# Two weight panels split earlier in a chain of two transformer blocks: a fifth query panel ahead of the first norm's root, a second memory panel ahead of the compressions' activation

## The reference

```python
def _rmsnorm(x, g):
    xf = x.astype(jnp.float32)
    y = xf * lax.rsqrt(jnp.mean(xf * xf, axis=-1, keepdims=True) + RMS_EPS)
    return (y * g.astype(jnp.float32)).astype(x.dtype)

def _compress(kv, pos, w1, w2):
    ...
    blocks = kv[:, idx] + pos[None, None, :, None, :]
    hid = jax.nn.gelu(jnp.einsum('bnlgd,lde->bnge', blocks, w1))
    return jnp.einsum('bnge,ed->bngd', hid, w2)

def _nsa_mixer(h, w_in, gate_b, cmp_pos, cmp_w1, cmp_w2):
    proj = h @ w_in
    q, kc, vc, ks, vs, kw, vw, gl, q_mem = _split(
        proj, [MIX_WIDTH] + [KV_WIDTH] * 6 + [3 * MIX_HEADS, MEM_WIDTH])
    ...
    kc_b = _compress(kc, cmp_pos[0], cmp_w1[0], cmp_w2[0])
    vc_b = _compress(vc, cmp_pos[1], cmp_w1[1], cmp_w2[1])

def _mem_attention(q_mem, mem_n, w_kv):
    k, v = jnp.split(mem_n @ w_kv, 2, axis=-1)
    ...

def first_block(x, mem, ...):
    for i in range(DEPTH):
        hn = _rmsnorm(x, norm1[i])
        mn = _rmsnorm(mem, norm_mem[i])
        ...
```

## Time and profile before

| what | us |
|---|---|
| median of 3 runs | 2215.55 |
| the 3 runs | 2217.01, 2210.09, 2215.55 |
| the profiled execution | 2217.38 |
| its span in the trace | 2215.6 |
| TensorE busy in the span | 2087.2 (94%) |
| VectorE busy | 1132.5 (51%) |
| ScalarE busy | 829.7 (37%) |
| GpSimd busy | 275.7 (12%) |

### The profile page before, as it was taken

One profiled execution on the slowest core, in us unless ns is written; L12 is line 12 of the kernel. 1 busy time (PEld: TensorE's weight loads), 2 busy tenths in 40 slices (PEclk: granted clock), 3 DMA queues, 4 the chain that ended last, 5 costly groups with the idle time before them and its releaser, 6 DMA issues.

```text
span 2215.6 us, 36210 instructions
## 1 busy us (share of the span) xinstructions
PE 2087.2 (94%) x15473; PEld 1136.2 (51%) x15617; DVE 1132.5 (51%) x1744; ACT 829.7 (37%) x1350; POOL 275.7 (12%) x343
## 2 busy tenths in 40 slices
PE   6988989999999999899999999999998989999998
PEld 3556554444444344689844444454565435444444
DVE  4866764544423457655545454333746465555221
ACT  4334764322322574332242223333435335322122
POOL 2221331000001110222210000011012123000000
PEclk9999999999999999999999999999999999999999
DMA  5442002433223311100024332331420021333220
GB/s 138 129 140 58 2 1 77 114 104 105 95 87 102 96 58 59 39 23 4 4 72 112 103 95 91 128 124 58 133 76 20 20 76 41 112 102 107 95 95 38
DMA packets 203843, 173.61 MB, mean 78 GB/s; under 512 B 20416, under 2 KB 179332, under 8 KB 203684
## 3 DMA queue, kind: packets, MB, share of 16 engines
q1 hardware_dynamic: 202778, 170.34, 25.2%
q10 hardware_dynamic: 906, 0.96, 0.2%
HBM read 169.18 MB, written 2.10 MB: 77 GB/s over the span
## 4 chain that ended last, share of the span: by engine, by line
PE 81%; DVE 8%; ACT 6%; issue 3%; POOL 1%; ACTq 0%; DMA 0%; DVEq 0%; POOLq 0%
PE banks L1142 45%; PE banks L1189 17%; PE banks L1464 5%; PE banks L1243 1%; ACT w_hi L1750 1%; PE banks L1476 1%; DVE w_lo L2317 1%; PE banks L1263 1%; PE banks L1204 1%; PE banks L1221 1%; PE banks L1652 1%; ACT arena L1852 1%; PE banks L1576 1%; POOL arena L990 1%; ACT arena L2151 1%
## 5 line engine op out<-in xcount | busy, mean ns | idle before, releaser
L1142 PE MATMUL banks<-arena,w_hi 128*128 128x512 bf16 (+3 forms) x2099 | 613.9, 373 | 7.8 <-DVE arena L2337 5.3
L2317 DVE TENSOR_TENSOR w_lo<-wring,w_hi 128x2048 bf16<-128x2048 f32 (+3 forms) x162 | 357.5, 2208 | 466.7 <-ACT w_hi L1750 463.0
L1750 ACT ACTIVATE w_hi<-wring 128x2048 f16<-128x2048 f32 (+3 forms) x162 | 294.8, 1822 | 442.4 <-PE banks L1189 255.3
L1142 PE MATMUL banks<-arena,w_lo 128*128 128x512 f16 (+1 forms) x1080 | 403.3, 373 | 3.2
L1189 PE MATMUL banks<-arena,w_hi 128*128 128x512 f16 (+1 forms) x1179 | 353.7, 379 | 2.2 <-DVE arena L2609 1.1
L1142 PEld LDWEIGHTS banks<-arena,w_hi 128*128 128x128 f16 x2160 | 211.0, 98 | 253.8 <-DVE arena L2337 8.2
L990 POOL TENSOR_TENSOR arena<-arena,ntmp 128x512 f32<-128x512 f32 (+1 forms) x79 | 101.9, 1290 | 1252.3 <-ACT ntmp L1780 1246.0
L1189 PE MATMUL banks<-arena,w_lo 128*128 128x512 f16 x608 | 230.4, 379 | 2.0
L1142 PE MATMUL banks<-h_hi,w_hi 128*128 128x512 f16 (+1 forms) x576 | 221.0, 384 | 9.8 <-DVE w_lo L2317 8.4
L1142 PE MATMUL banks<-h_hi,w_lo 128*128 128x512 f16 (+1 forms) x576 | 220.1, 382 | 2.2 <-issue 0.2
L1142 PE MATMUL banks<-h_lo,w_hi 128*128 128x512 bf16 (+1 forms) x537 | 205.4, 382 | 0.0
(11 more groups left out here) (404 smaller groups left out, 2737.1 us busy)
## 6 DMA issues: line engine op xcount, KB each, us to landing
wring<-in_w_ffn_in SPq DMA_DIRECT2D x88, 512.0 KB, 4.8
wring<-in_w_ff SPq DMA_DIRECT2D x32, 1024.0 KB, 5.2
wring<-in_w_ffn_out SPq DMA_DIRECT2D x20, 1024.0 KB, 5.0
wring<-in_rw_w_in SPq DMA_DIRECT2D x11, 1024.0 KB, 5.1
wring<-in_w_in SPq DMA_DIRECT2D x11, 1024.0 KB, 5.0
wring<-in_nsa_w_in SPq DMA_DIRECT2D x7, 1024.0 KB, 5.1
wring<-in_w_mem_kv SPq DMA_DIRECT2D x4, 1024.0 KB, 5.3
wring<-in_w_o SPq DMA_DIRECT2D x4, 1024.0 KB, 5.0
```

The lines of the kernel that those rows point to most:

```text
L1142: last = mm(v, p[0], p[1], start=(i == 0), stop=(i == len(prods) - 1))
L1750: A(w_hi[:, at[0] % NSPLIT, 0:w["size"]], wring[:, w["slot"], 0:w["size"]], ACT.Copy).then_inc(split_hi, 1)
L2317: V.tensor_tensor(w_lo[:, sl, 0:w["size"]], wring[:, w["slot"], 0:w["size"]], w_hi[:, sl, 0:w["size"]], ALU.subtract).then_inc(split_lo, 1)
```

## The change

The fifth query panel (split 4) is brought ahead of the root on both engines: ScalarE's `split_to(NBANK - 1)` ahead of `root(n1a)` becomes `split_to(NBANK)`, and VectorE gets a `split_to(NBANK)` ahead of its wait for `d_root`. The fifth query tile is computed in bank 7, and is put in `own_bank`, the list of tiles that don't wait in `opened`. The second memory panel (split 9) is brought ahead of the compressions' gelu, on ScalarE and on VectorE.

```diff
                 t, mm, v = feature_tile(w, 0, P, hT, "v")
+                if len(nsa_jobs) == NBANK:
+                    t.bank, v = 7, bank[7][:]
+                    mm = [(v, mm[0][1])]
                 nsa_jobs.append((t, mm, [x[:, gp * 3 + r, :] for x in qT], v, qscale[:, gp * 3 + r:gp * 3 + r + 1]))
...
-        own_bank = [conv_jobs[0][0]]
+        own_bank = [nsa_q[NBANK][0], conv_jobs[0][0]]
...
             act.wait_ge(cols_ready, 1)
-            split_to(NBANK - 1)
+            split_to(NBANK)
             root(n1a).then_inc(d_root, 1)
...
             prepare(mem_norm[1], lambda k: None)
-            split_to(mem_jobs[0][0][0].split)
+            split_to(mem_jobs[0][0][0].split + 1)
             for j in range(2):
                 act.wait_ge(gelu_in, j + 1)
...
                 last.then_inc(cmp_pos, 1)
+            split_to(NBANK)
             dve.wait_ge(d_root, n1a["r"] + 1)
             plain(nsa_q)
...
-            split_to(mem_jobs[0][0][0].split)
+            split_to(mem_jobs[0][0][0].split + 1)
             for j in range(2):
                 t = cmp_hid[j]
```

## The result

| what | us |
|---|---|
| kernel before, median of 5 runs | 2213.29 (2210.09 to 2217.01) |
| changed kernel, median of 5 runs | 2200.18 (2199.02 to 2205.11) |
| ratio, with its 95% interval | 0.9944 [0.9928, 0.9960] |
| profiled execution of the changed kernel, its span | 2201.43, 2199.4 |

The changed kernel is faster by 0.56%, 12.4 us of 2213. Two further series of 5 runs of the changed kernel, beside 24 and 21 of before, gave 0.9958 [0.9945, 0.9970] and 0.9960 [0.9947, 0.9973]. All 15 runs of it have a mean of 2202.45 (2199.02 to 2207.49), all 65 of before that were taken for this study 2212.90 (2209.14 to 2217.78): a difference of 10.4 us, uncertain by 1.8.

The account below looks back on a forecast made before the run. TensorE, busy 94% of the span, was taken to bound with two stops over 6 us, VectorE pacing between them. Gains 3.3 + 5.8 less 0.9 for clock gave 8.2 us: 2215.55 - 8.2 = 2207.4, range 2202 to 2213.

Parts of the forecast that it names:

- What bounds, and the order of pacing: TensorE's matmuls and stops bound; VectorE paces 68.28 to 89.24 us, TensorE from 123.40 on.
- First gain: Split 4 ahead of the root: VectorE starts the compression stretch earlier, 3.3 us gained.
- the second stop: TensorE's 6.35 us wait for `w_lo` of split 9, ahead of the first layer's memory value tile.
- Second gain: Split 9 ahead of the gelu: the second layer's first key tile starts 5.8 us earlier.
- The clock, -0.9: Deduction of 0.9 us for a possible 1.2 GHz stretch behind the gap ahead of the second layer's key tile.
- first stop: TensorE's 6.32 us wait for `w_lo` of split 4, ahead of the fifth query tile.
- The base, 2215.55: Median of the kernel before's three runs, spanning 6.9 us, from which the gain was subtracted.
- (1) Half the gain lost: Longer low stretch at the first compression tile, another behind the second gap, late panel: gain 3.9 us, 2211.7; chance 0.20.
- (2) Doesn't reach the end: Downstream low stretches, attention's lead or the next wait eat the gain: 0 to 3 us, 2214; chance 0.10.
- (3) A late landing: Second memory panel lands late, holding ScalarE, gelu and root; landing at 119 would give 2224; chance 0.03.
- (4) More than expected, 11.1: Early load, no low level after either gap, one downstream low stretch gone: gain 11.1 us, 2204.5; chance 0.07.

Follow-up runs that it names:

- the first part alone: Kernel before plus split 4 ahead of the root on both engines and the fifth query tile in bank 7, split 9 unmoved: ratio 0.9981.
- the bank alone: Kernel before with only the fifth query tile in bank 7 and its entry in `own_bank`, no split moved: ratio 0.9996.
- the split alone: Kernel before with split 4 ahead of the root on both engines, the fifth query tile left in bank 1: ratio 0.9985.
- the second part alone: Kernel before with only split 9 moved ahead of the gelu on ScalarE and VectorE: ratio 0.9978.
- before, with idle matmuls: Kernel before with 24 and 26 more matmuls, results unread, filling TensorE's two long stops, no wait moved: ratio 0.9976.
- one split further: Changed kernel with split 10 also ahead of the gelu on both engines: ratio 0.9971 against the kernel before.

## Why the prediction missed by little: point by point

**What bounds, and the order of pacing: right.** VectorE fills the compression stretch (20.51 of 20.98 us) as before, and its row at 64.24 shows no wait for TensorE. Behind the second stop TensorE is busy for all of 74.00 us.

**First gain: right.** Forecast 3.3; the trace shows 3.3, and the first part alone gave 4.2 [2.2 to 6.2 by its interval]. The gap ahead of the sixth tile was to be 2.7 and is 2.77. It did bring the low level to part of the sixth tile (0.63 us for a 512-column matmul from 52.06 to 54.62, where 0.38 is usual), and as forecast VectorE's chain hid it.

**Second gain: right.** Forecast 5.8, in the trace 6.0, alone 4.9 by the runs (2.7 to 7.1). The landing wait was to be 0.6 and is 0.57; the gelu starts 2.4 us behind the end of rest 8 for 2.6; the gap ahead of the second layer's key tile was to be 1.9 and is 1.71. Only the length of the low stretch that it removes was taken from too few rows (under "The clock"). By the Trainium skill, SBUF — State Buffer, section "SBUF: two separate sides", rest 9 might have been held behind a GpSimd selection. It wasn't: ScalarE released it, it started 0.19 us behind rest 8 and took 2.29 us. GpSimd's pair of selections, which started behind it, took 2.45 us, for 0.52 beside the gelu's operations; that agrees with the section, by which the one that starts second waits:

```profile
100.86 2.45 POOL L1016 TENSOR_SCALAR_AFFINE_SELECT masks<-masks 64x32 f32<-64x32 f32 x2
...
104.83 0.52 POOL L1016 TENSOR_SCALAR_AFFINE_SELECT masks<-masks 64x32 f32<-64x32 f32 x2
```

**The clock, -0.9: wrong, the first step that failed.** It was meant for a low stretch behind the second gap. Neither the trace above nor those of the two repeats (gaps of 1.92 and 1.49 us) has one there; the windows from the key tile on for 74 us show 1.00 in all three. It also left out that the low stretch which the change removes has no fixed length. I took the value tile's 6.6 us, 1.4 over the 5.2 of the full level, from one trace. Behind the same stop it takes 6.82 us with the first part alone, 7.89 with the bank alone, and 7.88 with the split alone:

```profile
112.66 0.37 PE L1142 MATMUL banks<-w_hi,arena 128*128 128x256 f16 x1 [6.35 <-DVE w_lo L2317]
...
120.54 0.38 PE L1142 MATMUL banks<-arena,w_hi 128*128 128x256 f16 x2
```

So it costs 1.4 to 2.7 us, 2.1 on the mean of these four traces. Without the deduction the sum is 9.1, with the trace's second gain 9.3, with this mean some 10.0; the runs say 10.4, uncertain by 1.8.

Nothing behind the second stop is shown to add to it. Each trace cut at the second layer's first key tile:

| kernel | the key tile starts at, us | from there to the span's end, us |
|---|---|---|
| before | 123.40 | 2092.2 |
| the bank alone | 123.67 | 2087.0 |
| the split without the bank | 120.54 | 2087.0 |
| the first part alone | 119.62 | 2087.4 |
| before, with idle matmuls | 119.77 | 2084.5 |
| the second part alone | 116.98 | 2086.5 |
| the changed kernel, three traces | 113.39, 113.92, 113.16 | 2086.0, 2089.1, 2086.2 |

The lead of 10.0 us is there at the key tile. Counted from the root, without what the starts differ by, it is 9.3 to 10.4 us (79.24 us in before and 80.20 with the bank alone, for 69.77 to 70.17 in the changed kernel's three), and that is all of the 10.4 of the runs. Behind it the changed kernel's three traces average 2087.1 us, no less than the kernels that keep one or both of the old stops; the trace of before is the one that stands apart. The mean granted clock is higher in the changed kernel, 0.9849 over 15 runs against 0.9822 over 60 of before, but that lies ahead of the key tile. The windows up to it, of before and of the changed kernel, and one of before's first stop:

```profile
0.00:123.40 123.40, 93.66 (x463) 58.21 (x468) 78.77 (x107) 47.95 (x77) 40.47 (x118) 0.90 0.51 131
0.00:113.39 113.39, 91.73 (x468) 57.39 (x468) 76.02 (x105) 48.52 (x78) 35.67 (x100) 0.95 0.53 133
44.20:50.40 6.20, 0.00 (x0) 0.00 (x0) 3.38 (x5) 4.01 (x8) 0.00 (x0) 0.80 0.00 0
```

A clock of 0.90 over 123.40 us is 12.3 us short of full, 0.95 over 113.39 is 5.7: the 6.7 between them are 0.003 of the span, all of the difference. Part of it is in the stops themselves, where the clock is already low (0.80) and TensorE has nothing to run.

**The base, 2215.55: the step that cost most.** I took the median of three runs as the place of the kernel before. Among 65 runs it lies high: their mean is 2212.9, and 8 of them are at 2215.5 or more. The three later series were run on three chips, with means of 2212.1, 2213.1 and 2213.4 for before. The profiled execution of before, 2217.38, is higher still, which is why the two traces differ by 16.2 us and not by 10: of the 6.2 us that come up behind 123.40, some 5 belong to that one execution (2092.2 for 2087.0 in the table). The repeats' traces lead it by 12.6 and 16.2 us at the end, and by 9.5 and 10.2 at the key tile.

The miss of 7.2 us thus comes apart into 2.7 from the base (2215.55 - 2212.90), 2.2 from the gain (10.4 for 8.2: 0.9 the deduction for the clock, 0.2 the second gain, some 0.7 the low stretch that is longer in other traces, and 0.4 within what the runs leave uncertain), and 2.3 since the first five runs lie below the mean of all fifteen (2202.45 - 2200.18), which is luck of the draw. My range left the first and the last out: it was made from the cases' sizes around a base that I treated as known to a us, where three runs that span 6.9 us say it isn't.

**The rivals.** (1) Half the gain lost: the longer low stretch, the second gap's and a late landing all failed to come. (2) Doesn't reach the end: it does, 10.0 us at 123.40 were not given back. (3) A late landing: 0.57 us in the changed kernel; the mechanism is real, as one split further shows. (4) More than expected, 11.1: nearest to the 12.4 of the first five runs, by another way; the load landed no earlier, the first gap did bring the low level, and no low stretch downstream is shown to have dropped out. Of its conditions only the second gap at the full level came true.

## What to carry to other kernels

When an engine waits for a reduction of another, move into that wait the operation that its consumer will want next, and then look for the same operation in the queue of every engine that makes it: here the split's new place gave the gain, and the free bank nothing that could be told. Stop where the load of the moved step isn't certain to be there, because everything queued behind it, and every bank that this work frees, waits with it. Take the price of a low stretch from several traces, since one trace shows one length of it, and compare traces at the end of the changed stretch before the rest of a span is put down to a change. Before a gain of a few us is forecast as a time, learn how far runs of the old kernel spread, and put that into the range.

## What the runs showed of the hardware

The spread of one kernel's runs goes with TensorE's granted clock. Of 60 runs of before, by the mean clock of each:

| mean granted clock | runs | mean time, us |
|---|---|---|
| 0.980 | 3 | 2215.43 |
| 0.981 | 14 | 2215.18 |
| 0.982 | 22 | 2212.77 |
| 0.983 | 11 | 2211.33 |
| 0.984 | 9 | 2210.38 |
| 0.985 | 1 | 2211.53 |

A fit gives 1.4 us for each 0.001, where 0.001 of the span is 2.2 us. This holds within one kernel and doesn't price a change: the idle matmuls raise the mean clock by 0.0043 (0.9865 over 11 runs), of which some 0.004 lies ahead of the key tile (a clock of 0.97 over 119.77 us, 3.6 us short of full for 12.3), much of it in stops where the level costs nothing. Which stretches after a gap are granted 1.2 GHz differs from one execution to the next: a gap of 2.05 us ahead of 19.91 was followed by 3.4 us at the low level in before, while one of 1.55 us at the same place in the changed kernel wasn't, nor were its 1.71 us ahead of 113.39. How long the low level lasts differs too: 1.4 to 2.7 us of it at the value tile, behind stops of 6.35 and 6.54 us. The two rows of the changed kernel's windows at those places:

```profile
20.00:24.00 4.00, 4.00 (x21) 1.80 (x19) 3.80 (x6) 3.81 (x7) 0.00 (x0) 1.00 1.31 233
...
113.40:130.00 16.60, 16.60 (x217) 13.63 (x218) 12.13 (x19) 5.73 (x3) 9.64 (x25) 1.00 0.83 260
```
